# Packed attention steps, and four changed borders, in a hybrid encoder step on one core

## The chip, the cores and the metric

The program runs on one core of one Trainium2 chip. The metric is device time in microseconds (us) for one execution of the whole program. One execution was profiled; the others were only timed.

## The reference

One layer of a streaming encoder for 1024 prompt frames and 8 x 16 sample frames (T = 1152 columns) of width 1024, in f32. What matters here:

```
z = rmsnorm(x, g_mix) @ w_in            # cq, ckv, kpe, rq, rk, rv, rg, sq, sk, sv
o_mla = softmax(q k^T * scale, chunk-causal) @ v          # 8 heads, 96 wide
o_ret = retention(rq, rk, rv); ret_y = head_norm(o_ret) * silu(rg)
# stick-breaking, 4 heads of 64:
z_ = q k^T / 8;  before = k_pos < q_pos
log_keep = where(before, log_sigmoid(-z_), 0)
a = where(before, exp(log_sigmoid(z_) + reverse_exclusive_cumsum(log_keep)), 0);  o_sb = a @ v
x = x + concat(o_mla, ret_y, o_sb) @ w_out
x = x + memory_attend(rmsnorm(x), 256 memory tokens, 4 heads of 128)
x = x + conv_ffn(rmsnorm(x));  y = rmsnorm(x)
```

The sample frames have caches of 512 past frames (MLA latents, stick-breaking keys and values) and their own memory keys and values.

## The kernel before

Everything lies features by frames in on-chip memory: 8 or 18 blocks of 128 features, each over 1152 frames. A product with weights is made as three fp32r products (high part with high part, high with low, low with high), in chunks of 384 frames (`CH`, `NCH` = 3); a projection of one block is 3 chunks of 24 products. Each engine has its own list of instructions, in an order written out by hand; semaphores join the lists. Weights stream in 512 KB slots through two buffers: SyncE (SP) loads, GpSimd (POOL) splits into high and low parts (L749, L752), TensorE (PE) multiplies (L1751 in `split_products`, L1829 in `first_projection`), VectorE (DVE) evacuates.

**Input projection.** 18 blocks in the order `IN_ORDER`; block n goes to banks 3(n mod 2) + c. `z_chunk` (L1263, L1268) evacuates. The last four blocks hold the stick-breaking queries and values of one head each. After the last block, `stick_breaking_tokens` (L1960) transposes the values by tiles into banks 4 to 7.

**Prompt attention.** `STEPS` lists steps for two heads at a time: 2 x 8 stick-breaking steps `("sb", pair, tile)`, then four MLA passes of 8 steps `("mla", pass, tile)`, with four sample steps `("sbs", ...)` set between MLA steps by `SB_S_AFTER`. Step j handles the 128 queries of tile j against the 128(j + 1) keys up to it, so that its width grows from 128 to 1024 columns. S[0] and S[1] (two PSUM banks each, banks 0 to 3) hold the scores of the first and the second head; banks 4 and 5 take the transposes, bank 6 the output, bank 7 the projections. In iteration t:

- TensorE: scores (L1976 sb, L1979 mla, L1992 and L1995 sample) and the transposes of step t - 1 (L2009), first head, then second head; then a projection chunk for a later pass (L2049, L2052, L2056, L2061, `project_chunk`); the values of step t - 2 (L2031, sample L2026); further chunks. `STEP_CHUNKS` says which chunks stand in which iteration: eleven for each pass, made during the pass before, and those of pass 0 during stick-breaking. The chunks share bank 7, so each waits until the one before is evacuated.
- VectorE: for sb a mask on the last 128 columns (L1430), then, when ScalarE has written the sigmoids, a reversed running product (scan, L1456) and a product (L1459); for mla a memset of the hidden corner (L1445), the row maximum (L1447), a reciprocal and a scaling (L1466, L1468); copies of transposes (L1477), query chunks (L1490).
- ScalarE: two sigmoids (L931, L932; sample L940, L941) or the exponential (L949), copies of the transposes (L959), outputs into `mixed` (L967, L973, L977), other chunks (L1001, L1002, L1006).

`kbuf` (the 1 - sigmoid part) is single for each head, `prob` double. In iteration 2 (`KPE_STEP`) the rotary key is turned (L1421, ScalarE L913, L1424). SP loads the mask `hide`, then `rope_pe` and `w_pass` after the last input block, stores sk and sv, loads the sample caches (L658, L659; each waits until the values of the sample step before are done), and later the MLA latents.

**Sample MLA.** Eight steps, one for each sequence (L2095, L2096, L2104, L2113; VectorE L1537 to L1547, ScalarE L1044 to L1059), then the head products L2119 and a copy into `mixed` (L1063).

**Output projection.** ScalarE rounds the eight blocks of `mixed` (L1072), VectorE makes the remainders (L1552), and `first_projection` (L1829) takes them block by block as they come.

**Memory attention.** Twelve steps (`N_MEM`): eight prompt tiles with four heads (scores L2152, values L2174), four pairs of sample sequences (scores L2160, values L2182: 16 products of 16 columns), transposes L2194. VectorE: maximum L1592, remainder of the output L1598, copy L1606, reciprocal and scaling L1609, L1612. ScalarE: exponentials L1101, copies L1111, rounding L1135, sample queries L1126 into `qm_pair`, which VectorE clears once (L1586) before the loop. `memory_output(m, c)` makes block m, chunk c of the projection behind it from 12 products; two chunks stand in iteration N_MEM - 1, and 22 after the loop.

```python
            pe.wait_ge(g_evac, G_MO)
            pe.wait_ge(qm_zero, 1)
            for n in range(N_MEM + 2):
```

## Time and profile before

| | |
|---|---|
| runs, us | 1861.46, 1866.43, 1856.43 (median 1861.46) |
| profiled execution: its own time | 1855.89 us |
| its span | 1854.1 us, mean granted TensorE clock 0.976 |
| TensorE busy | 1779.7 us (96%), 10471 products |
| VectorE, ScalarE, GpSimd busy | 1084.6 (58%), 552.7 (30%), 490.6 us (26%) |
| chain that ended last | TensorE 87%, VectorE 8%, ScalarE 3%, issue 2% |
| input projection ends | 325.6 us |
| first output product | 720.5 us |
| memory attention begins | 877.4 us |
| last memory output product | 1007.9 us |

A group in the profile is a line, an engine, an operation and its tiles, with count, busy time, the mean of one and the idle time before it. The chain of waits is followed back from the last instruction. Products overlap, so that a busy TensorE is not one at its peak. An f32 product counts as two records, an fp32r product or a transpose as one.

### The profile page before, as it was taken

How to read it: one execution, taken by the hardware profiler on the slowest of the kernel's cores; microseconds unless marked ns; L12 is line 12 of the kernel's file. 1: busy time of each engine (PE TensorE's matmuls, PEld its weight loads, DVE VectorE, ACT ScalarE, POOL GpSimd, SP SyncE). 2: the span in 40 equal slices, each digit the busy share in tenths (PEclk: the TensorE clock that was granted, in tenths of full speed). 3: DMA queues.
4: the chain of work that ended last, by engine and by line, in shares of the span. 5: the costliest groups of instructions: out<-in, count | busy, mean ns of one | idle time of the engine just before them, and what ended most of it. 6: DMA issues, size and time to landing. Idle time of an engine off the chain costs nothing.

```text
span 1854.1 us, 26688 instructions
## 1 busy us (share of the span) xinstructions
PE 1779.7 (96%) x10471; PEld 1615.7 (87%) x10471; DVE 1084.6 (58%) x1519; ACT 552.7 (30%) x1037; POOL 490.6 (26%) x219
## 2 busy tenths in 40 slices
PE   7999999898998998999999999999999999999997
PEld 7998899455655757998899999999999999999987
DVE  7754365677445665443627766656555565565577
ACT  7211110566554644110513312121121121211234
POOL 2851121000000011433003433333333333233331
PEclk9999899899999999999989999999999999999999
DMA  5330110501111311331421111111111111111112
GB/s 212 92 109 12 60 41 17 159 10 48 58 46 46 119 47 41 133 123 38 190 110 46 35 46 45 45 34 45 45 35 44 45 45 34 45 45 34 46 44 102
DMA packets 34974, 119.29 MB, mean 64 GB/s; under 512 B 4944, under 2 KB 7984, under 8 KB 32464
## 3 DMA queue, kind: packets, MB, share of 16 engines
q1 hardware_dynamic: 32592, 108.76, 17.9%
q10 hardware_dynamic: 2304, 9.44, 1.5%
q8 instruction: 56, 0.92, 0.2%
q14 instruction: 22, 0.18, 0.0%
HBM read 100.73 MB, written 15.17 MB: 63 GB/s over the span
## 4 chain that ended last, share of the span: by engine, by line
PE 87%; DVE 8%; ACT 3%; issue 2%; DMA 0%; ACTq 0%; DVEq 0%; SPq 0%
PE scores L1751 33%; PE bank L1751 31%; PE scores L1979 3%; PE scores L1829 2%; PE bank L2009 2%; DVE kbuf L1456 2%; PE bank L2031 2%; PE bank L2049 2%; PE bank L2182 1%; PE bank L2026 1%; DVE prob L1459 1%; PE scores L1773 1%; PE scores L2160 1%; PE bank L1760 1%; PE scores L1992 1%
## 5 line engine op out<-in xcount | busy, mean ns | idle before, releaser
L749 POOL TENSOR_TENSOR w_hi<-w_raw,zero 128x1024 fp32r<-128x1024 f32 x96 | 186.9, 1947 | 1292.9 <-PE bank L1751 570.2
L1751 PE MATMUL scores<-act_hi,w_hi 128*128 128x384 f32 x976 | 330.5, 339 | 0.0
L1751 PE MATMUL scores<-act_lo,w_hi 128*128 128x384 f32 x976 | 328.7, 337 | 0.0
L1751 PE MATMUL scores<-act_hi,w_lo 128*128 128x384 f32 x976 | 328.7, 337 | 0.0
L752 POOL TENSOR_TENSOR w_lo<-w_raw,w_hi 128x1024 fp32r<-128x1024 f32 x96 | 250.1, 2606 | 7.6
L1751 PEld LDWEIGHTS scores<-act_hi,w_hi 128*128 128x128 f32 x976 | 184.2, 189 | 0.6 <-issue 0.2
L1751 PEld LDWEIGHTS scores<-act_lo,w_hi 128*128 128x128 f32 x976 | 184.2, 189 | 0.3 <-issue 0.2
L1751 PEld LDWEIGHTS scores<-act_hi,w_lo 128*128 128x128 f32 x976 | 184.1, 189 | 0.0
L1679 DVE TENSOR_TENSOR x<-bank,x 128x384 f32<-128x384 f32 x216 | 120.4, 558 | 103.6 <-PE bank L1751 103.6
L1751 PE MATMUL bank<-act_hi,w_hi 128*128 128x384 f32 x512 | 172.2, 336 | 0.0
L1751 PE MATMUL bank<-act_hi,w_lo 128*128 128x384 f32 x512 | 172.0, 336 | 0.0
L1751 PE MATMUL bank<-act_lo,w_hi 128*128 128x384 f32 x512 | 172.0, 336 | 0.0
L1653 DVE SCALAR_TENSOR_TENSOR conv<-ext,consts,conv 128x1168 f32<-128x1168 f32 x44 | 117.5, 2671 | 79.4 <-ACT conv L1152 79.4
L1751 PE MATMUL bank<-s_hi,w_hi 128*128 128x384 f32 (+2 forms) x454 | 153.0, 337 | 0.0
L1751 PE MATMUL bank<-s_lo,w_hi 128*128 128x384 f32 (+2 forms) x454 | 152.7, 336 | 0.0
L1751 PE MATMUL bank<-s_hi,w_lo 128*128 128x384 f32 (+2 forms) x454 | 152.6, 336 | 0.0
L1163 ACT ACTIVATE s_hi<-conv 128x1024 fp32r<-128x1024 f32 x20 | 21.2, 1061 | 344.1 <-DVE conv L1662 344.1
L2009 PEld LDWEIGHTS bank<-ident,prob 128*128 128x128 f32 x452 | 54.4, 147 | 51.8 <-DVE prob L1459 23.0
L1751 PEld LDWEIGHTS bank<-act_hi,w_hi 128*128 128x128 f32 x512 | 96.3, 188 | 0.2
L1751 PEld LDWEIGHTS bank<-act_lo,w_hi 128*128 128x128 f32 x512 | 96.3, 188 | 0.0
L1751 PEld LDWEIGHTS bank<-act_hi,w_lo 128*128 128x128 f32 x512 | 96.3, 188 | 0.0
L2009 PE MATMUL bank<-ident,prob 128*128 128x128 f32 x452 | 73.3, 291 | 15.6 <-DVE prob L1459 11.2
(341 smaller groups left out, 3377.7 us busy)
## 6 DMA issues: line engine op xcount, KB each, us to landing
w_raw<-wstream SPq DMA_DIRECT2D x108, 512.0 KB, 3.5
x_blk<-xT ACTq DMA_DIRECT2D x8, 576.0 KB, 4.6
x_mid<-x_blk ACTq DMA_DIRECT2D x8, 576.0 KB, 3.1
x<-x_mid SPq DMA_DIRECT2D x4, 1152.0 KB, 6.5
z<-cache_k SPq DMA_DIRECT2D x4, 1024.0 KB, 5.2
z<-cache_v SPq DMA_DIRECT2D x4, 1024.0 KB, 7.2
mk_c<-mk_c SPq DMA_DIRECT2D x4, 1024.0 KB, 11.5
mv_c<-mv_c SPq DMA_DIRECT2D x4, 1024.0 KB, 13.5
```

Source lines behind the costliest of these rows:

```text
L749: pool.tensor_tensor(w_hi[:, k], w_raw[:, k], zero[:].unsqueeze(2).to_broadcast([P, KB, P]), ALU.add).then_inc(w_rounded, 1)
L752: pool.tensor_tensor(w_lo[:, k], w_raw[:, k], w_hi[:, k].bitcast(F32), ALU.subtract).then_inc(w_split, 1)
L1163: act.activation(dst[:, 0:TP], conv[:, 0, 0:TP], ACT.Copy)
L1456: own_v(dve.tensor_tensor_scan(keep[:, ::-1], keep[:, ::-1], ones[:, 0:1].to_broadcast([P, width]), 1.0, ALU.mult, ALU.mult))
L1653: own_v(dve.scalar_tensor_tensor(c, ext[:, ab, 1:EXT - 1], conv_tap(m + NFF * ab, 1), c, ALU.mult, ALU.add))
L1679: dve.tensor_tensor(x[:, m, frames(c)], bank[6 + q % 2][:, 0:CH], x[:, m, frames(c)], ALU.add).then_inc(d_evac, 1)
L1751: mm = pe.matmul(out, w[:, k, at + kb], x(kb), start=first and kb == 0 and n == 0, stop=last and kb == n_kb - 1 and n == 2)
L1829: mm = pe.matmul(bank[c][:, 0:CH], w[:, 0, kb], x[:, kb, frames(c)], start=kb == 0 and n == 0, stop=kb == KB - 1 and n == 2)
L1979: mm = pe.matmul(S[hh][:, at:end], q_pass[i % 2][:, hh, tile(j)], k_pass[i % 2][:, hh, at:end], start=True, stop=True)
L2009: mm = pe.transpose(bank[4 + g % 2][:, tile(b)], prob[:, t % 2, hh, tile(4 * k + b)], ident[:])
L2031: mm = pe.matmul(bank[6][64 * hh:64 * hh + 64, 0:P], v, probT[:, t % 2, hh, tile(b)], start=b == 0, stop=b == j)
L2049: mm = pe.matmul(bank[7][:, 0:CH], w_pass[:, s, (2 * hh + kb) * P:(2 * hh + kb + 1) * P], z[:, Z_CQ + kb, frames(k)], start=kb == 0, stop= ...
```

## The change

Five things. (1) An attention step takes one or two tiles, up to 8 blocks of 128 keys: `PACKS` is (7), (6, 0), (5, 1), (4, 2), (3). A pair or a pass has 5 steps instead of 8. The tiles of a step lie side by side in S, and row maximum, exponential, scan, product and scaling are issued for each tile by itself; transposes, their copies, the mask and the memset for the step. The chunks and the sample steps are set anew, a chunk can also stand between the heads. (2) The first stick-breaking step is tile 3 of pair 0; its scores stand between chunks 0 and 1 of input block 16, whose banks become 6, 7 and 1. Its sigmoids lie in `kbuf0` and `prob0`, and `hide` is loaded ahead of the last input weights, into the place of `bd`. (3) Blocks 6 and 7 of `mixed` are rounded during the sample MLA, and the output projection starts with them. (4) The clearing of `qm_pair` moves into iteration 2 of the memory loop. (5) The value products of the four sample pairs are issued between the products of four chunks of the memory output, (0, 1), (1, 0), (0, 0), (1, 1).

```diff
-    return (0, 1, 4)[c] if n in RET_BLOCKS else 3 * (n % 2) + c
+    return (0, 1, 4)[c] if n in RET_BLOCKS else (6, 7, 1)[c] if n == NZ - 2 else 3 * (n % 2) + c
...
+MIX_ORDER = (6, 7, 0, 1, 2, 3, 4, 5)
+MIX_AFTER = {4: 6, 6: 7}
+MO_CHUNKS = [(0, 1), (1, 0), (0, 0), (1, 1)]
+MO_CHUNKS += [(m, c) for m in range(KB) for c in range(NCH) if (m, c) not in MO_CHUNKS]
...
-SB_S_AFTER = {(0, 4): 0, (1, 1): 1, (1, 6): 2, (2, 3): 3}
-STEPS = [("sb", p, j) for p in range(2) for j in range(NTILE)]
+PACKS = ((7,), (6, 0), (5, 1), (4, 2), (3,))
+SB_S_AFTER = {(0, 2): 0, (1, 0): 1, (1, 3): 2, (2, 1): 3}
+STEPS = [("sb", p, tiles) for p in range(2) for tiles in (PACKS[4:] + PACKS[:4] if p == 0 else PACKS)]
...
 for _n in range(NCK):
-    STEP_CHUNKS[3 + _n].append((0, _n))
+    STEP_CHUNKS[2 + _n // 2][_n % 2 + 1].append((0, _n))
     for _i in range(1, NP):
-        STEP_CHUNKS[FIRST[_i - 1] + min(7, (_n + 1) * 2 // 3)].append((_i, _n))
+        _steps = [_t for _t in range(FIRST[_i - 1], END[_i - 1]) if STEPS[_t][0] == "mla"]
+        STEP_CHUNKS[_steps[(_n + 1) // 3]][(_n + 1) % 3].append((_i, _n))
...
+        hide = Region(at_bd, 512)("hide", [P, P])
+        kbuf0 = Region(at_pair[0] + 17408, 4096)("kbuf0", [P, 2, 512])
+        prob0 = Region(at_pair[1] + 4608, 4096)("prob0", [P, 2, 512])
...
+                if slot == W_OUT - 1:
+                    sp.wait_ge(sum_used, Q_HEAD + 6)
+                    sp.dma_start(hide[:], io["before"][:, 1]).then_inc(hide_in, 16)
                 sp.wait_ge(w_split, slot - 1)
                 load_weights(slot)
...
             sp.wait_ge(w_used, W_OUT)
-            sp.dma_start(hide[:], io["before"][:, 1]).then_inc(hide_in, 16)
...
 # ScalarE
+            act.wait_ge(ret_done, 2)
+            for hh in range(2):
+                sb_sigmoids(0, hh)
+            act.wait_ge(w_used, W_OUT)
+            act.wait_ge(lora_normed, 3)
+            act.wait_ge(g_evac, NZ * NCH)
+            sb_sigmoids(1, 0)
+            stick_breaking_values(0)
+            stick_breaking_values(2)
+            copy_groups(0, 0)
+            stick_breaking_values(4)
+            sb_sigmoids(1, 1)
+            copy_groups(0, 1)
...
+                for n, (_, at, w) in enumerate(spans(t)):
+                    last = act.activation(prob[:, t % 2, hh, at:at + w], S[hh][:, at:at + w], ACT.Exp,
+                                          bias=neg_max[:, k + n:k + n + 1], accum_out=row_sum[:, k + n:k + n + 1])
...
+                    if b in MIX_AFTER:
+                        act.wait_ge(stored_skv, 128)
+                        round_mixed(MIX_AFTER[b])
...
-            for kb in range(KB):
-                act.activation(mix_hi[:, kb], mixed[:, kb], ACT.Copy).then_inc(mix_rounded, 1)
+            for kb in MIX_ORDER[2:]:
+                round_mixed(kb)
...
 # VectorE
+            dve.wait_ge(hide_in, 16)
+            z_chunk(NZ - 2, 0)
+            mask(0, 0)
+            mask(0, 1)
+            z_chunk(NZ - 2, 1)
+            finish(0, 0)
+            z_chunk(NZ - 2, 2)
+            finish(0, 1)
+            z_evacuate(NZ - 1)
+            for t in range(1, N_STEPS + 2):
...
                 if heads:
                     mask(t, 0)
+                if t == 1:
+                    stick_breaking_values(1)
+                    stick_breaking_values(3)
                 if copied:
                     copy_groups(t - 1, 0)
                 if heads == 2:
                     mask(t, 1)
+                for chunk in STEP_CHUNKS[t][0]:
+                    evacuate_chunk(*chunk)
                 if heads:
                     finish(t, 0)
                 if copied == 2:
                     copy_groups(t - 1, 1)
-                for chunk in STEP_CHUNKS[t][:1]:
+                for chunk in STEP_CHUNKS[t][1]:
                     evacuate_chunk(*chunk)
                 if heads == 2:
                     finish(t, 1)
...
+                if n == DB - 1:
+                    split_mixed(0)
+            for i in range(1, KB):
+                split_mixed(i)
...
-            for k in range(2):
-                dve.wait_ge(xb_out[k], 16 * KB // 2)
-            dve.memset(qm_pair[:], 0.0).then_inc(qm_zero, 1)
             for n in range(N_MEM + 3):
...
+                if n == 2:
+                    for k in range(2):
+                        dve.wait_ge(xb_out[k], 16 * KB // 2)
+                    dve.memset(qm_pair[:], 0.0).then_inc(qm_zero, 1)
                 if n < N_MEM:
                     dve.wait_ge(m_exp, n + 1)
...
 # TensorE
+            input_chunk(NZ - 2, 0)
+            pe.wait_ge(g_evac, NCH * (NZ - 2))
+            for hh in range(2):
+                scores(0, hh)
+            input_chunk(NZ - 2, 1)
+            input_chunk(NZ - 2, 2)
+            input_block(NZ - 1)
+            pe.wait_ge(g_evac, NCH * (NZ - 1))
+            scores(1, 0)
+            pe.wait_ge(g_evac, NCH * NZ)
+            for g in range(4):
+                value_tokens(g)
+            scores(1, 1)
+            pe.wait_ge(sv_copied["act"], 2)
+            value_tokens(4)
+            pe.wait_ge(sv_copied["dve"], 1)
+            for hh in range(2):
+                transposes(0, hh)
...
+            for t in range(2, N_STEPS + 2):
                 for hh in range(2):
                     if t < N_STEPS and hh < n_heads(t):
                         sample_scores(t) if STEPS[t][0] == "sbs" else scores(t, hh)
                     if 1 <= t <= N_STEPS and hh < n_heads(t - 1):
                         transposes(t - 1, hh)
-                for chunk in STEP_CHUNKS[t][:1]:
-                    project_chunk(*chunk)
+                    for chunk in STEP_CHUNKS[t][hh]:
+                        project_chunk(*chunk)
                 if t >= 2:
                     values(t - 2)
...
-            first_projection(W_OUT, G_OUT - 2 * NCH, mix_split, 0, mix_hi, mix_lo)
+            first_projection(W_OUT, G_OUT - 2 * NCH, mix_split, 0, mix_hi, mix_lo, MIX_ORDER)
...
+            def sample_values(c, i):
+                if i < 5:
+                    sample_value(c, 2 * i)
+                    sample_value(c, 2 * i + 1)
+                else:
+                    sample_value(c, i + 5)
...
-            pe.wait_ge(qm_zero, 1)
...
+                        memory_output(*MO_CHUNKS[c - NTILE], lambda i: sample_values(c, i))
...
-                if n == N_MEM - 1:
-                    memory_output(0, 0)
-                    memory_output(0, 1)
-            for n in range(2, KB * NCH):
-                memory_output(n // NCH, n % NCH)
+            for m, c in MO_CHUNKS[DB // 2:]:
+                memory_output(m, c)
```

`spans(t)` gives for each tile of a step its number, its first column in S and its width; `between` is called behind each of the first eleven of a chunk's twelve products. `sample_value(c, i)` issues product i of the sixteen.

## Rows read from the trace of the kernel before

**Rows 1.** Windows: stretch, length, busy us (x) of PE, PEld, DVE, ACT, POOL, PEclk, DMA, GB/s

```profile
325.60:385.20 59.60, 49.32 (x238) 26.79 (x238) 44.52 (x60) 34.13 (x71) 0.00 (x0) 0.84 0.44 124
...
385.20:443.50 58.30, 52.61 (x333) 33.13 (x333) 40.60 (x59) 39.89 (x91) 0.00 (x0) 0.90 0.13 46
...
443.50:636.60 193.10, 179.80 (x1177) 120.56 (x1177) 101.81 (x249) 104.32 (x246) 0.00 (x0) 0.97 0.15 51
...
636.60:675.90 39.30, 36.75 (x296) 24.83 (x294) 28.52 (x64) 22.05 (x55) 8.96 (x4) 1.00 0.35 121
...
926.90:1007.90 81.00, 79.83 (x456) 78.04 (x455) 39.67 (x53) 19.72 (x27) 13.89 (x6) 0.89 0.23 83
```

**Rows 2.** Chain of waits in stick-breaking: start us, us, what

```profile
366.79 0.22 DVE scores L1430
...
368.79 2.04 DVE kbuf L1456
...
385.21 1.97 PE bank L2009 x8
...
437.62 1.97 PE bank L2009 x8
```

**Rows 3.** Chain of waits in the memory attention and its output

```profile
875.50 1.78 DVE qm_pair L1586
...
926.97 3.46 PE scores L2160 x16
...
935.25 5.70 PE scores L2160 x16
...
940.96 3.48 PE bank L2182 x32
...
944.70 4.17 PE scores L1751 x24
...
953.04 6.72 PE bank L2182 x32
...
960.50 5.81 PE scores L1751 x24
```

**Rows 4.** Groups by form, 325.6 to 720.5 us: VectorE and ScalarE in stick-breaking

```profile
L1456 DVE TENSOR_TENSOR_SCAN kbuf<-kbuf,ones 128x1024 f32<-128x1024 f32 x4 | 9.1, 2286 | 3.6 <-ACT prob L932 3.6
...
L1430 DVE TENSOR_TENSOR scores<-scores,hide 128x128 f32<-128x128 f32 x32 | 8.9, 295 | 10.1 <-PE scores L1976 10.0
...
L1459 DVE TENSOR_TENSOR prob<-prob,kbuf 128x1023 f32<-128x1023 f32 x4 | 4.9, 1224 | 0.1
...
L932 ACT ACTIVATE prob<-scores 128x1024 f32<-128x1024 f32 x4 | 4.2, 1045 | 0.0
```

**Rows 5.** Chain of waits in the MLA passes, TensorE

```profile
492.64 1.73 PE scores L1979 x4
...
499.79 1.29 PE bank L2049 x4
...
507.23 1.71 PE scores L1992 x4
...
509.38 1.34 PE scores L1992 x3
...
529.44 4.41 PE bank L2026 x40
...
627.06 0.77 PE bank L2009 x7
...
637.93 1.90 PE bank L2031 x32
```

**Rows 6.** DMA issues, 488 to 500 us: KB each, us to landing

```profile
z<-cache_v SPq DMA_DIRECT2D x1, 1024.0 KB, 7.2
```

**Rows 7.** Chain of waits at the output projection

```profile
715.12 1.12 PE bank L2119 x16
...
720.51 14.61 PE scores L1829 x72
```

More of the change, by code:

```diff
@@ L1520, in _ @@
                     finish(t, 1)
-                for chunk in STEP_CHUNKS[t][1:]:
+                for chunk in STEP_CHUNKS[t][2]:
                     evacuate_chunk(*chunk)
@@ L1746, in _, with split_products @@
         def _(pe):
-            def split_products(out, k, at, n_kb, hi, lo, first=True, last=True, weights=(w_hi, w_lo)):
+            def split_products(out, k, at, n_kb, hi, lo, first=True, last=True, weights=(w_hi, w_lo), between=None):
                 for kb in range(n_kb):
```

264 lines of the change are left out of this document (141 added, 123 removed).

## The prediction

> **What bounds the kernel now.** I read the windows by stage first, then the chain of waits in order of time, then the groups by form for the price of one instruction, and last the DMA issues. In the windows the reader is to see that TensorE is busy nearly everywhere, so a gain has to come from one of three places: TensorE idle, TensorE running at its lower level, or TensorE busy with work that could lie under something else. Outside the stretch from 325.6 to 1007.9 us the change touches nothing.
>
> The stretch splits in four. (a) Stick-breaking, 325.6 to 443.5 us: TensorE is idle for 10.3 us and then 5.7 us, and its mean granted clock is 0.84 and 0.90 [rows 1]. The chain there runs through VectorE: mask, then two sigmoids on ScalarE, then scan and product [rows 2]. (b) The MLA passes with four sample steps between them, 443.5 to 675.9: 232.4 us, 216.6 of them busy, clock 0.97 and 1.00. (c) The seam between the sample MLA and the output projection, around 715 to 735. (d) The memory attention and its output projection, to 1007.9: TensorE counts as busy for 79.8 of the last 81.0 us, but at a mean clock of 0.89 [rows 1]; the sample scores of a step take 3.46 us in one place and 5.70 in the next, and one group of value products 3.48 and then 6.72 [rows 3]. So in (d) it is the clock and the short products that cost.
>
> **Stick-breaking, packed.** A pair of heads goes through 36 blocks of 128 keys for each head either way. Before, these are 8 steps; after, 5 (8, 8, 8, 8 and 4 blocks). Columns, scans, products and score matmuls stay the same in number. One full width costs VectorE 2.286 (scan) + 1.224 (product) us and ScalarE 1.045 us for each of two sigmoids [rows 4]. For a pair: 36 blocks are 4.5 full widths, times two heads, times 3.51, is 31.6 us; the extra instructions of narrow tiles (about 0.3 us for each tile and head beyond 4.5, an estimate from the 0.295 us of a 128-column operation [rows 4]) bring 33.8. Each step also has an opening that VectorE cannot fill: mask 0.3, hand-over 0.1, the first head's two sigmoids; the row pair 366.79 to 368.79 shows 2.0 us at 896 columns [rows 2]. Eight openings are 8 x 0.4 + 2 x (4.5 x 1.045 + 3.5 x 0.17) = 13.8 us, five are 2.0 + 9.6 = 11.6. So the sum is 47.6 before, 45.4 after. But the second pair took 385.21 to 437.62, 52.4 us [rows 2]: 4.8 us more than the sum, the latency of its narrow first steps behind the widest step of the pair before. Steps of even width should lose most of that: 6 us gained in the second pair, from the first scan on.
>
> The first pair: its 512-column step moves between chunks of block 16. What moves: on TensorE two heads of scores, 2 x 0.87 = 1.7 us, which now lengthen the input projection; on VectorE two masks, two scans and products (2 x 1.9 us), among evacuations of 1.1 us every 4.2 us, so hidden; on ScalarE four sigmoids and the table load, where it was waiting anyway. On SP the mask's load is moved ahead of the last weight load: 64 KB, hidden because that load is waiting for its split anyway; if it were not, TensorE would wait for the last weights by the load's few us at most. What is left behind the projection is the last evacuation (1.1 us), the 1024-column step's scores and the value transposes, then a rotary key of 4 us on VectorE as before. I work the first pair out as 45.4 - 5.5 (the moved step) + 3.5 (start) + 4 (rotary) + 6 x 0.55 (query evacuations) + 1.7 = 52.4 against 59.6 now: 7 us. The chunks of pair 0 now start one step earlier and wait for the stores of sk and sv; I put that at 0 to 3 us. A second charge: TensorE at half speed just after the border, which now meets a full step instead of narrow ones; 0 to 5 us. Stage (a): 6 + 7 - 2 = **11 us**, bounds 0 and 16.
>
> **The MLA passes, packed.** TensorE's own work in a full step is scores 2 x 1.73, sixteen transposes at 0.11 and values 1.90 = 7.1 us; a pass is 4 x 7.1 + 3.6 = 32.0 [rows 5]. A query chunk is 1.29; the five others of a pair 0.86 or less by their columns; eleven make 11.8, for three pairs 35.4. A sample step is 1.71 + 1.34 + 5 x 0.11 + 4.41 = 8.0, four are 32 [rows 5]. Sum 4 x 32.0 + 35.4 + 32 = 195 us against 232.4 measured: 37 us are latency and clock. Narrow steps (2 to 6 blocks) have too little TensorE work to cover mask, exponential and scaling of the same step; a packed step has 7.1 us of it. What stays: with three chunks in a step, the second waits for VectorE to evacuate the first behind the second head's mask, about 1.2 us, twice a pass, 7 us in all; the last pass without chunks is near VectorE's own 6.5 to 7.5 us a step, 3 us; sample steps with their two table loads of 1.28 us, 1 to 2 us each instead of about 5; clock and hand-overs 4 to 6. That leaves about 216: **16 us**, bounds 4 (only the sample steps gain) and 28.
> What is late next: the cache of a sample step is loaded after the values of the one before, and lands 7.2 us after its issue [rows 6]. Now only one step lies between the two, 8.8 to 10 us of TensorE's work by the prices above. It fits by 1 to 2 us; if it does not, up to 3 us for each of three loads.
>
> **The seam before the output projection.** Now the products start at 720.51, after the head products of 715.12 (1.12 us), the copy, and the first rounding and its remainder [rows 7]. After, two of eight blocks are ready and TensorE can start at 716.3. Two blocks last 2 x 1.56 = 3.1 us (12.5 us for eight at full clock); the third is ready at 720.4 as the first is now; six more last 9.4, so the end is 729.9 instead of 720.51 + 14.61 = 735.12: **5 us**, bounds 3 and 6. The two roundings move into the sample MLA on ScalarE (1.15 us each), which has over 2 us free in a step of 4.6; the remainder (1.37) behind VectorE's last scaling may delay a copy, 0 to 0.5 us.
>
> **Memory attention.** The memset of 1.78 us that TensorE waits for [rows 3] goes; it comes back in VectorE's queue in the third step, where VectorE and ScalarE set the pace. I charge it in full there; left is that TensorE starts without the stop: **1 us**, 0 to 3. Then the sample values: 16 products of 16 columns cost 3.48 us at full clock, 0.109 for each of 32 weight loads, and 12 products of 384 columns 2.08 (24 in 4.17) [rows 3]. Interleaved, a weight load can lie under each long product: 11 x 0.109 = 1.2 us a group, 4.8 for four. The low clock now costs (5.70 - 3.46) + (6.72 - 3.48) + (5.81 - 4.17) = 7.1 us [rows 3]. With long products in between, I expect some two thirds of that back: **10 us** together, bounds 0 (loads do not overlap between short and long, clock as before) and 13. Two chunks already filled this place, so only two are new there. Weights: the first block is split before the loop begins; VectorE's sums keep their order, with the counts moved.
>
> Sum: 11 + 16 + 5 + 1 + 10 = **43 us**. The profiled execution took 1855.9 us for a span of 1854.1; it is at the lower end of the runs (median 1861.5), so 1813 by its own time, and about 1817 to 1818 beside the median. A change within 0.5%, 9 us, would not be told from none.
>
> **A rule against it.** The same transposes cost 0.11 us each (seven in 0.77) and, behind the widest stick-breaking step, 0.25 (eight in 1.97) [rows 2, 5]: they run at either level of the clock, 1.2 or 2.4 GHz, and the lower one came where TensorE had waited for VectorE's scan. The Trainium skill (TensorE: Matmul & The Clock Gate, Part 4: PE-mode transpose) says that transposes do not count as TensorE activity and that the full clock does not engage for them. The trace disagrees as to the full clock; whether they count, no row here shows. By that rule the packed stick-breaking steps, with their transposes in long runs between waits, would invite the lower level, which leads to the slower rival below.
>
> **The rivals.**
> 1. *Forecast*, 1807 to 1828, chance 0.50.
> 2. *The latency stays*: packed steps only join waits, because masks, chunk evacuations and table loads stand in the same order on VectorE and ScalarE, and the memory loop keeps its low clock. Stage (a) 6, (b) 7, seam 4, memory 5: 22 us, about 1840. For it: VectorE is in the chain of the wide steps too [rows 2]. Chance 0.25.
> 3. *More*: every cover holds, 14 + 25 + 6 + 14 = 59 us, 1802. Against it: the waits between chunks. Chance 0.12.
> 4. *The gain goes*: the caches land late (9 us), the stores hold the first chunks (3), nothing in memory: about 1856. Chance 0.06.
> 5. *Slower: TensorE's clock falls in the packed stick-breaking steps.* At 1.2 GHz a full step needs 2 x 7.1 + 2 us of chunks = 16.3 against VectorE's 11.2: +5 us in each of eight steps, 41 us; with the four full steps of the last pass (14.2 against 7.6) 26 more. Net 43 - 67: 24 us slower, 1885. It decides once the mean clock in such a step is under (7.1 + 1.2)/11.2 = 0.74. Against it: 0.84 and 0.90 now, and packed steps give TensorE more work between waits. Chance 0.07.
> That the change does nothing can be excluded: the steps, and the order of products, are written out.
>
> **How the numbers follow.** The likeliest case gives 1817. Low 1797 takes in the third case; high 1846 takes in the second; outside are the last two and the edges. Faster by over 0.5%: 0.50 + 0.25 + 0.12, less a little at the edge, 0.86; within, 0.07; slower 0.07.
>
> **What would show it.** Stick-breaking from the end of the input projection to the last scan should be about 99 us instead of 112, with a step of 1024 columns every 10 to 11.5 us and the mean clock not under 0.84. The MLA stage should be 216 us or less, with TensorE idle under 8 us. The first output product should start within 0.2 us of the head products' end, with one wait of about 1 us before the third block. The interleaved groups should take about 4.4 us each and no stretch among them show a clock near 0.5. I am wrong if a sample score waits for the cache's DMA, if a packed step has TensorE at the lower level and VectorE idle, or if a group of short and long products takes 5.5 us or more.

## The result, and the profile after

The changed kernel takes 1840.9 us (median; 1836.8 to 1844.3) against 1863.7 for the kernel before in the same runs: ratio 0.9893, 95% interval 0.9867 to 0.992. By the ratio that is some 20 us faster: inside the range, but less than half of the 43 that the sum gave. The profiled execution took 1842.4 us for a span of 1840.6; the kernel before had a span of 1854.1. These 13.5 us are made up so: the stretch of the change gained 21.1; the input projection was already 3.3 us behind where the change first touches it; and what follows the memory output, where nothing was changed, took 4.3 more, at a lower mean clock (0.94 over the last 150 us against 0.98).

The windows by stage of the changed kernel (columns as in [rows 1]):

```profile
330.16:425.59 95.43, 84.64 (x536) 54.84 (x535) 74.00 (x89) 61.82 (x108) 0.00 (x0) 0.95 0.32 93
425.59:661.17 235.58, 216.64 (x1502) 149.70 (x1502) 134.50 (x277) 121.23 (x290) 8.80 (x4) 0.99 0.19 67
...
700.40:715.34 14.94, 14.04 (x89) 13.55 (x90) 9.27 (x9) 7.04 (x7) 0.00 (x0) 1.00 0.25 80
...
854.79:907.36 52.57, 46.72 (x291) 41.96 (x292) 33.54 (x45) 27.39 (x116) 4.24 (x2) 0.94 0.42 171
907.36:990.13 82.77, 81.67 (x456) 79.79 (x455) 36.44 (x52) 19.66 (x27) 16.42 (x6) 0.88 0.23 81
```

The first line answers to the first two of [rows 1]: the clock is 0.95 instead of 0.84 and 0.90. The second answers to the next two: 235.6 us for passes and sample steps against 232.4, TensorE idle for 18.9 us against 15.8. (These windows begin with the first scores of the passes, which now start 1.0 us before the last stick-breaking product ends and started 5.9 after it before. So the table below counts the passes from that product.) The last one answers to the last: 82.8 us against 81.0, at 0.88 against 0.89. Set against the terms, each as lengths of the stage:

| term | forecast gain, us | measured, us |
|---|---|---|
| stick-breaking, to its last product | 11 | 112.0 to 96.4, less 1.3 that the projection grew: 14.3 |
| passes, from that product | 16 | 238.3 to 234.6: 3.7 |
| seam, from the head products to the end of the first output block | 5 | 20.0 to 14.9: 5.1 |
| memset | 1 | 2.2 gained before the loop, 2.4 lost in it: -0.2 |
| interleaving and its clock | 10 | -1.9 |

The stick-breaking product and scan are VectorE's (L1534 and L1529 here); "to" and "from" it mean its end. Three stretches of the chain of waits in the passes show what the second term met (start us, us, what):

```profile
438.66 1.74 PE scores L2081 x6
...
440.48 0.17 DVE scores L1516
...
440.72 0.97 issue
441.69 0.28 DVE neg_max L1519
441.97 0.47 DVE q_pass L1568
...
442.49 0.59 PE bank L2152
...
498.17 0.60 PE bank L2111 x4
...
499.40 0.82 ACT L991
...
500.70 0.70 ACT prob L991
501.40 0.60 ACT prob L992
...
502.03 1.50 DVE prob L1529
...
503.55 0.83 DVE prob L1534
...
504.43 0.93 PE bank L2111 x5
...
640.94 1.14 issue
642.08 2.50 DVE prob L1545
644.57 0.60 DVE probT L1555
...
645.28 3.82 DVE prob L1545 x2
...
649.14 0.68 PE bank L2111 x4
```

First, TensorE waits 2.08 us (440.40 to 442.49) for VectorE to evacuate a query chunk behind mask and maximum; this is in the chain six times. In four of the six, transposes run under 0.87 us of it, and 1.2 us are idle; in the other two TensorE is idle for 2.1. That is 9.2 us in all. Second, a sample step: 5.66 us from 498.77 to 504.43 for table load, two sigmoids, scan and product. Third, the end of the last pass: 9.93 us from 639.23 on. There GpSimd is at work, in the timeline of its engine (start us, us, what):

```profile
641.88 2.47 POOL L812 TENSOR_TENSOR w_lo<-w_raw,w_hi 128x1024 fp32r<-128x1024 f32 x1
644.32 2.01 POOL L809 TENSOR_TENSOR w_hi<-w_raw,zero 128x1024 fp32r<-128x1024 f32 x1
646.40 2.47 POOL L812 TENSOR_TENSOR w_lo<-w_raw,w_hi 128x1024 fp32r<-128x1024 f32 x1
```

And the groups by form give the price of the same scaling, up to 636 us and after (busy us, mean ns):

```profile
L1545 DVE TENSOR_SCALAR prob<-prob,row_sum 128x384 f32<-128x384 f32 x6 | 2.5, 415 | 0.0
...
L1545 DVE TENSOR_SCALAR prob<-prob,row_sum 128x384 f32<-128x384 f32 x2 | 5.0, 2492 | 0.0
```

A scaling of 384 columns that costs 415 ns takes 2492. The one at 642.08 ends at 644.57, just after GpSimd's operation of 641.88 has ended at 644.35. In the memory attention, two lines of the chain and the group after them:

```profile
871.63 1.76 DVE qm_pair L1705
...
907.36 3.46 PE scores L2296 x16
910.99 0.35 PE bank L2268 x4
911.34 0.27 PE scores L1849
...
916.21 0.27 PE scores L1849
916.70 3.46 PE scores L2296 x16
```

The memset is back in the chain, in the third iteration, for 1.76 us. The woven group of 16 short and 12 long products lasts from 910.82 to 916.48, 5.66 us at full clock. Apart they are 3.48 + 2.08 = 5.56 by [rows 3]; 4.4 was forecast.

### The profile page after: what moved, and what is told of

The parts are those of the page before. It is cut to its first block, busy times and chain, and to the rows that moved or that the text cites. A ratio compares the mean times of both kernels' runs of the same rounds, so it can differ in the third digit from the quotient of the medians.

```text
span 1840.6 us, 26432 instructions
## 1 busy us (share of the span) xinstructions
PE 1771.5 (96%) x10471; PEld 1621.2 (88%) x10471; DVE 1079.3 (59%) x1459; ACT 538.9 (29%) x977; POOL 493.7 (27%) x219
## 4 chain that ended last, share of the span: by engine, by line
PE 89%; DVE 6%; ACT 2%; issue 2%; DMA 0%; ACTq 0%; DVEq 0%; SPq 0%
PE scores L1849 33%; PE bank L1849 32%; PE scores L2081 3%; PE bank L2111 2%; PE bank L2134 2%; PE scores L1929 2%; PE bank L2152 2%; PE scores L2078 1%; DVE kbuf L1529 1%; PE bank L2128 1%; PE scores L1873 1%; PE bank L1860 1%; PE scores L2296 1%; PE scores L2094 1%; PE bank L2268 1%
## 5 line engine op out<-in xcount | busy, mean ns | idle before, releaser
L1849 PE MATMUL scores<-act_hi,w_hi 128*128 128x384 f32 x960 | 325.2, 339 | 0.0
L1849 PE MATMUL scores<-act_lo,w_hi 128*128 128x384 f32 x960 | 323.5, 337 | 0.0
L1849 PE MATMUL scores<-act_hi,w_lo 128*128 128x384 f32 x960 | 323.4, 337 | 0.0
L1849 PE MATMUL bank<-act_hi,w_hi 128*128 128x384 f32 x528 | 177.7, 337 | 0.0
L1849 PE MATMUL bank<-act_hi,w_lo 128*128 128x384 f32 x528 | 177.4, 336 | 0.0
L1849 PE MATMUL bank<-act_lo,w_hi 128*128 128x384 f32 x528 | 177.4, 336 | 0.0
L1751 DVE SCALAR_TENSOR_TENSOR conv<-ext,consts,conv 128x1168 f32<-128x1168 f32 x44 | 117.5, 2671 | 79.4 <-ACT conv L1227 79.4
L1753 DVE SCALAR_TENSOR_TENSOR conv<-ext,consts,conv 128x1168 f32<-128x1168 f32 x44 | 84.3, 1916 | 5.7 <-DVE conv L1751 3.0
L1849 PEld LDWEIGHTS bank<-s_hi,w_hi 128*128 128x128 f32 x454 | 85.4, 188 | 0.4
```

The source lines that it names most:

```text
L1751: own_v(dve.scalar_tensor_tensor(c, ext[:, ab, 1:EXT - 1], conv_tap(m + NFF * ab, 1), c, ALU.mult, ALU.add))
L1753: dve.scalar_tensor_tensor(c, ext[:, ab, 2:EXT], conv_tap(m + NFF * ab, 2), c, ALU.mult, ALU.add).then_inc(conv_done, 1)
L1849: mm = pe.matmul(out, w[:, k, at + kb], x(kb), start=first and kb == 0 and n == 0, stop=last and kb == n_kb - 1 and n == 2)
```

## The experiments

All but the last three change the changed kernel in one respect. The stages are taken from one profile of each, by the same starts each time: the passes from the last stick-breaking product (VectorE's) to the last value product of the passes, the memory part from the first sample value to the last product of the projection behind the memory output. The kernel before has 238.7 and 89.8. Where the text gives gains in us for a whole kernel "by the ratios", it is the difference of two ratios times the 1859 us of the kernel before in those runs.

| kernel | ratio to before, 95% | passes, us | memory part, us |
|---|---|---|---|
| changed | 0.9893 (0.9867 to 0.992) | 234.4 | 91.5 |
| e7, passes single | 0.9915 (0.9896 to 0.9934) | 234.7 | 91.4 |
| e8, stick-breaking single | 0.996 (0.9946 to 0.9974) | 232.7 | 91.4 |
| e9, roundings late | 0.9925 (0.9896 to 0.9954) | 233.9 | 96.3 |
| e4, split late | 0.9856 (0.9825 to 0.9887) | 228.1 | 96.0 |
| e5, chunk slots | 0.9839 (0.9796 to 0.9883) | 227.8 | 96.0 |
| e6, sample places | 0.9852 (0.9814 to 0.9889) | 229.8 | 96.3 |
| e3, memset early | 0.9869 (0.9831 to 0.9906) | 235.5 | 96.0 |
| e1, values alone | 0.9858 (0.9837 to 0.9878) | 234.3 | 87.8 |
| e2, blocks | 0.9896 (0.9877 to 0.9915) | 232.2 | 86.5 |
| b1, all, values alone | 0.9774 (0.9747 to 0.9801) | 217.5 | 89.5 |
| b2, all, blocks | 0.9782 (0.9758 to 0.9806) | 217.7 | 91.3 |
| e10, b1's memory part and split, passes single | 0.9849 (0.9817 to 0.9882) | 233.3 | 89.8 |

**Passes in single tiles.**

```diff
-SB_S_AFTER = {(0, 2): 0, (1, 0): 1, (1, 3): 2, (2, 1): 3}
+SB_S_AFTER = {(0, 4): 0, (1, 1): 1, (1, 6): 2, (2, 3): 3}
...
-    for _k, _tiles in enumerate(PACKS):
+    for _k, _tiles in enumerate((_j,) for _j in range(NTILE)):
...
-        STEP_CHUNKS[_steps[(_n + 1) // 3]][(_n + 1) % 3].append((_i, _n))
+        _slots = STEP_CHUNKS[FIRST[_i - 1] + min(7, (_n + 1) * 2 // 3)]
+        _slots[2 if _slots[1] else 1].append((_i, _n))
```

> The changed kernel with the MLA passes back in single tiles (8 steps a pass), their chunks and the sample steps where they stood before; stick-breaking stays packed. Measured is the stretch from the last stick-breaking product to the end of the last pass's values (238.3 us in the kernel before, 234.6 in the changed one). Theory A (the packed steps save hardly anything, since TensorE's own work of some 195 us now lies wholly on the chain and about 40 us of waits remain, while before some 30 us of that work lay under the waits): the stretch becomes 235 to 240 us, the kernel 0 to 5 us slower than the changed one, so 1841 to 1846. Theory B (the forecast: packing is worth 16 us there, and something else in the changed kernel, such as the steps' new place behind stick-breaking, took it away again): the stretch grows by 10 us or more, the kernel to about 1851 to 1857.

The stretch is 234.7 us in single tiles and 234.4 packed, and the ratios differ by 0.0022, 4 us, with intervals that overlap. As the change places its chunks and sample steps, packing is worth between nothing and 4 us: theory A.

**Stick-breaking in single tiles.**

```diff
-STEPS = [("sb", p, tiles) for p in range(2) for tiles in (PACKS[4:] + PACKS[:4] if p == 0 else PACKS)]
+STEPS = [("sb", p, (j,)) for p in range(2) for j in ((3, 7, 0, 1, 2, 4, 5, 6) if p == 0 else range(NTILE))]
...
-    STEP_CHUNKS[2 + _n // 2][_n % 2 + 1].append((0, _n))
+    STEP_CHUNKS[3 + _n][1].append((0, _n))
```

> The changed kernel with stick-breaking back in single tiles (8 steps a pair; the 512-column step still first and still between the last two blocks of the input projection, the 1024-column one behind it, then 128, 256, ... in order); the MLA passes stay packed. Measured is the time from the end of the input projection to the last stick-breaking product: 112.0 us in the kernel before, 96.4 in the changed one. Theory A (the forecast's working: the packing gives 6 us in the second pair and, with the moved step worth most of the first pair's 7, another 1 to 4 in the first): 103 to 107 us here, the kernel 7 to 10 us slower than the changed one. Theory B (the moved step alone did it, the packed steps only join waits): 96 to 99 us, 0 to 3 slower. Theory C (packing did nearly all): 108 to 112, 12 to 16 slower.

From the projection's end to the end of the last product it is 109.2 us (329.5 to 438.7), and the kernel is 12.5 us slower than the changed one (0.0067 of 1859). That is theory C, not the forecast's A: of the 15.6 us that the change gained here, packing gives 12.8 and the moved step the rest. The windows of the two, changed kernel and then this one:

```profile
332.00:426.00 94.00, 83.21 (x532) 54.46 (x532) 73.26 (x88) 62.18 (x110) 0.00 (x0) 0.95 0.32 93
```

```profile
331.40:437.40 106.00, 92.09 (x526) 55.33 (x526) 75.85 (x99) 67.70 (x151) 0.00 (x0) 0.90 0.30 92
```

VectorE's own work is 2.6 us less when packed; the other 9.4 us are its idle time, 30.1 against 20.7. TensorE's mean clock is lower as well in single tiles, 0.90 against 0.95. How much of the idle time goes back to that, and how much to the latency of narrow steps, isn't separated here.

**Roundings of two blocks late.**

```diff
-MIX_AFTER = {4: 6, 6: 7}
+MIX_AFTER = {}
...
-            for kb in MIX_ORDER[2:]:
+            for kb in MIX_ORDER:
...
-                if n == DB - 1:
-                    split_mixed(0)
-
-            for i in range(1, KB):
+
+            for i in range(KB):
                 split_mixed(i)
```

> The changed kernel with the early rounding of two blocks undone: blocks 6 and 7 are rounded and split behind the head products with the rest, in the same order of products. The seam from the end of the sample MLA's head products to the end of the first output block's products was 20.0 us before and 14.9 after. Theory A (the forecast: those two blocks give TensorE 3.1 us to work on while the third is made ready, and the start is 1.2 us of rounding and 1.4 of remainder earlier): 19 to 20.5 us again, the kernel 4 to 6 us slower than the changed one. Theory B (the gain came from elsewhere, such as the clock): 15 to 17 us, within 2.

From the head products' start to the start of the last product of the first block it is 20.2 us (699.84 to 720.0) instead of 14.6, and the kernel is 6 us slower: theory A. The order alone is worth nothing; the two early blocks are worth the forecast's 5 us.

Part of these 5 us is the clock. The 72 products of the first block take 15.15 us here and 14.61 in the kernel before, and at full clock 12.5. The window of the kernel before:

```profile
720.51:735.12 14.61, 14.61 (x73) 14.61 (x74) 9.67 (x9) 5.85 (x6) 0.00 (x0) 0.86 0.07 27
```

In both kernels the lower level came while TensorE stood idle, for 4.3 us, before the first product; in the changed kernel, where it starts at once, the window shows 1.00. So some 3 us of the 5.1 are the wait, and 2.1 (14.61 - 12.5) the clock.

**GpSimd's split late.**

```diff
             sp.wait_ge(q_evac, evacuated(NP - 1, NCK - 1, "dve"))
+            sp.wait_ge(p_ready, N_ITEMS)
```

> The changed kernel with one wait added on SP's queue: the weights of the output projection are loaded only once VectorE has scaled the last pass, so GpSimd splits them beside the sample MLA and not beside the last packed steps. In the changed kernel's chain VectorE's two scalings of the last full step take 3.67 and 3.81 us while GpSimd splits, and TensorE waits 9.93 us for them and runs at the lower level afterwards. Theory A (GpSimd slows VectorE): the scalings take under 1.2 us, the wait at the end of the last pass is 3 to 5 us, and the kernel is 6 to 9 us faster than the changed one, so about 1833, provided the weights are still in time for the output projection. Theory B (the wait is the last pass's own latency, since no chunks fill it): the scalings stay over 3 us or the wait stays over 8, and the total within 2 us. Theory C (the weights come too late): the first output products start 2 us or more later after the head products.

6.3 us off the passes, and 6.9 off the kernel by the ratios: theory A. Of the 9.93 us at the end of the last pass no wait over 1 us is left, where theory A had left 3 to 5. In its groups by form from 628 us on the scaling has its price again:

```profile
L1546 DVE TENSOR_SCALAR prob<-prob,row_sum 128x512 f32<-128x512 f32 x2 | 1.0, 487 | 0.1
L1546 DVE TENSOR_SCALAR prob<-prob,row_sum 128x384 f32<-128x384 f32 x2 | 0.8, 414 | 0.0
```

The output projection starts no later behind the last value product (41.1 us both times).

**Chunk slots.**

```diff
-        STEP_CHUNKS[_steps[(_n + 1) // 3]][(_n + 1) % 3].append((_i, _n))
+        _at = ((0, 1), (0, 2), (1, 1), (1, 2), (2, 1), (2, 2), (3, 0), (3, 1), (3, 2), (4, 0), (4, 1))[_n]
+        STEP_CHUNKS[_steps[_at[0]]][_at[1]].append((_i, _n))
```

> The changed kernel with the chunks of a pass in other slots: no packed step has a chunk between its two heads' scores and transposes and another right behind in the place where the second has to wait for VectorE to evacuate the first. In the changed kernel this wait of 2.08 us is in the chain six times, 0.87 of it being transposes that have to run anyway: 1.2 us net, 7 in all. Theory A (the wait is taken out): six waits fewer in the chain, the stretch of the passes 5 to 7 us shorter, the total too. Theory B (the latency moves: the mask and the exponential of the second head end the next wait instead, or the last chunk's evacuation delays the next pass's first scores): the stretch within 2 us of the changed kernel's 234.6.

6.6 us off the passes: theory A. None of the six waits of 2.08 us is left. In two of the passes a wait of 3.68 us stands where two of them were (4.18 in a third), as at 438.89 in its chain:

```profile
438.97 0.18 DVE scores L1517
...
439.17 1.29 DVE neg_max L1520 x2
...
441.45 0.60 DVE probT L1556
442.05 0.48 DVE q_pass L1569
...
442.57 1.56 PE bank L2153 x4
```

The chain alone would not show a gain, as the longer waits are as long in sum. But TensorE works under them; under the one shown run eight transposes, a chunk and 16 value products, and 0.5 us is idle. In all, TensorE's idle time in the stretch is 12.6 us (227.8 less 215.2 busy), against 18.6 (234.4 less 215.8).

**Places of the sample steps.**

```diff
-SB_S_AFTER = {(0, 2): 0, (1, 0): 1, (1, 3): 2, (2, 1): 3}
+SB_S_AFTER = {(0, 1): 0, (1, 1): 1, (2, 0): 2, (2, 3): 3}
```

> The changed kernel with the four stick-breaking sample steps further from each other and from the pass borders: behind the second, second, first and fourth steps of the passes rather than the third, first, fourth and second. What is measured is whether the caches' loads or the neighbours' width set the wait at these steps. In the changed kernel they cost 1 to 2 us of TensorE idle each net of its own work. Theory A (place matters: behind full steps only): 2 to 5 us faster. Theory B (two table loads and a 640-column scan make the wait wherever the step stands): within 2 us.

4.6 us off the passes, at the upper end of theory A. Two steps still show the full wait of 5.67 us (555.88 and 602.54), the other two now none over 1.5.

**Memset in the first iteration.**

```diff
-                if n == 2:
+                if n == 0:
```

> The changed kernel with VectorE's zeroing of the query pairs in the first iteration of the memory loop, where VectorE waits for the exponentials anyway, rather than in the third. In the changed kernel the chain runs through this operation for 1.76 us in the third iteration. Theory A (it stands in VectorE's queue where VectorE sets the pace): the operation is out of the chain and the stretch from the loop's first scores to the last prompt values 1.5 to 2 us shorter (51.5 in the changed kernel, 49.6 to 51.5 in others of its kind, by the clock). Theory B (VectorE had time): the same stretch, another operation in the chain in its place.

Theory A: the operation is out of the chain, and the stretch from first scores to last prompt values is 48.2 us, against 51.5 in the changed kernel and 49.1 before. Kernels that leave the memset in the third iteration have 49.6 to 51.5, by the clock, so less than the whole 3.3 us is its own. The total can't show it: its four runs scatter over 18 us (1825.7 to 1844.0).

**Sample values by themselves.**

```diff
-MO_CHUNKS = [(0, 1), (1, 0), (0, 0), (1, 1)]
+MO_CHUNKS = []
...
-                        memory_output(*MO_CHUNKS[c - NTILE], lambda i: sample_values(c, i))
+                        for i in range(11):
+                            sample_values(c, i)
...
+                if n == N_MEM - 1:
+                    memory_output(0, 0)
+                    memory_output(0, 1)
...
-            for m, c in MO_CHUNKS[DB // 2:]:
+            for m, c in MO_CHUNKS[2:]:
```

> The changed kernel with the last of its parts undone: the sample values of the memory attention run by themselves again, the chunks of the memory output in plain order, two of them in the last iteration as before. Measured is the stretch of the four groups, 80.9 us before, 82.8 after, and the clock in it, 0.89 before. Theory A (the interleaving saves nothing: what the weight load of a short product gains under a long one, the long one's own load loses, and the lower clock only shifts): the stretch is 80 to 82 us, the kernel 1 to 3 us faster than the changed one. Theory B (the forecast: interleaving saves 4.8 us of loads and some clock, hidden by a loss elsewhere in the stretch): the stretch is 85 us or more, the kernel 3 us or more slower.

3.7 us off the memory part, and the kernel 6.5 us faster than the changed one by the ratios: theory A, and beyond its 1 to 3. In the profiles, 2.8 us more lie in the input projection and 3.0 behind the memory part, where the two kernels are alike, so the edit is shown for the 3.7 only.

**Values and chunk as blocks.**

```diff
-                        memory_output(*MO_CHUNKS[c - NTILE], lambda i: sample_values(c, i))
+                        for i in range(11):
+                            sample_values(c, i)
+                        memory_output(*MO_CHUNKS[c - NTILE])
```

> The changed kernel with the same order of chunks and of sample values, but each set of 16 short products ahead of its chunk of 12 long ones, as two blocks, rather than woven together. At full clock the two together are 3.48 + 2.08 = 5.56 us by the rows of the kernel before; woven they took 5.66. Theory A (no load is hidden on balance): 5.5 to 5.7 us for the two at full clock, and the stretch of four groups within 1 us of the changed kernel's 82.8, the total within 1 us. Theory B (weaving does save loads, 0.109 us for each of 11): 6.7 us for the two at full clock or 4 to 5 us more for the stretch. Theory C (short products in one run draw the lower clock, which the weaving prevents): the clock of the stretch falls below the changed kernel's 0.86, and the stretch grows by 2 us or more with the pair still at 5.56 where the clock is full.

Its chain, one group at full clock:

```profile
907.24 3.48 PE bank L2268 x32
910.72 2.19 PE scores L1849 x12
```

5.67 us in blocks, 5.66 woven: on loads, weaving saves nothing. The memory part is 5 us shorter than woven in the profile, so none of the three theories has it whole: A is right on the loads and wrong on the stretch, and C has the clock the wrong way round. The total doesn't bear the 5 us out: the six runs go from 1830.9, the profiled one, to 1841.9, and the ratio is that of the changed kernel.

Over all profiles: the eight kernels with woven groups have a memory part of 91.4 to 96.3 us, the six without (the kernel before among them) 86.5 to 91.3. The longest stretch at the lower level of the clock, 0.50, in the changed kernel, in e4, in e1 and in e2 (windows):

```profile
929.50:950.00 20.50, 19.84 (x77) 19.02 (x77) 1.77 (x5) 0.72 (x3) 0.00 (x0) 0.50 0.15 47
```

```profile
914.20:944.90 30.70, 29.60 (x117) 28.34 (x116) 2.76 (x9) 1.17 (x5) 0.00 (x0) 0.50 0.21 80
```

```profile
926.60:940.30 13.70, 12.53 (x51) 12.20 (x50) 2.36 (x6) 1.19 (x4) 0.00 (x0) 0.50 0.37 134
```

```profile
925.60:932.40 6.80, 6.37 (x24) 5.90 (x24) 0.49 (x2) 0.45 (x2) 0.00 (x0) 0.50 0.00 0
```

TensorE is busy nearly throughout the memory part, so each microsecond at the lower level costs half of one. With that half taken off, nothing is left of the differences (us):

| kernel | memory part | longest at 0.50 | all at 0.50 | part less half of that |
|---|---|---|---|---|
| changed (woven) | 91.4 | 20.5 | 20.5 | 81.2 |
| e4 (woven) | 96.0 | 30.7 | 30.7 | 80.7 |
| before | 89.8 | 10.2 | 17.1 | 81.3 |
| e1, values alone | 87.8 | 13.7 | 13.7 | 81.0 |
| e2, blocks | 86.5 | 6.8 | 10.2 | 81.4 |
| b2, all, blocks | 91.3 | 6.8 | 20.5 | 81.0 |

All 14 profiles have 80.6 to 81.4 us in the last column. So the order of short and long products costs or saves nothing by itself that these 0.8 us would show; what differs is the time at the lower level, 20.5 to 30.7 us in the eight woven kernels and 10.2 to 20.5 in the six others. e2 and b2 have the same order and differ by 10 us of it, so one profile of a kernel doesn't settle its share.

**All together.** The edits of e3, e4, e5 and e6, with those of e1 (b1) or of e2 (b2):

> The changed kernel with five of its choices altered at once: the interleaving undone, the memset in the memory loop's first iteration, GpSimd's split of the output projection's first weights behind the last scaling, the chunks in their new slots, the stick-breaking sample steps at their new places. Alone, the split, the slots and the places took 6.3, 6.6 and 4.6 us off the stretch of the passes (234.4 us from the last stick-breaking product to the last value product), and the undone interleaving took 3.6 us off the end of the memory attention. If they add up, the stretch is 217 us, which is what the forecast gave the packed passes (216 or less from the first scores), the memory part is 5 us shorter, and the kernel 20 us faster than the changed one: 1820 (ratio to the kernel before 0.979). If they overlap (the same wait taken out twice, the next one behind it): 226 to 229 us for the stretch and 1829.

> The same kernel as the one before, but with sample values and chunk as two blocks in each of the four groups, rather than all sample values by themselves and two chunks in the last iteration. Theory A (what matters is TensorE's clock in the stretch, and the less of the 16-column products stand close together the better): 0 to 5 us faster than the other. Theory B (the shorter the short products' stretch in all, the less time at the lower level): 2 to 6 us slower than the other, as the two stood to each other on the changed kernel (1838 against 1833).

They add up: the passes take 217.5 and 217.7 us (234.4 less 6.3, 6.6 and 4.6 is 216.9), and the medians are 1818.0 and 1818.5 us beside 1859.3 for the kernel before, 22 us faster than the changed kernel for b1. Between the two there is no difference that the runs can tell. One cost came back in b1: from the last value product to the first output product 46.1 us instead of 41.1. The split now meets the first scaling of the sample MLA, as chain and GpSimd's timeline show:

```profile
649.63 2.39 DVE prob L1648
...
649.32 2.34 POOL L814 TENSOR_TENSOR w_lo<-w_raw,w_hi 128x1024 fp32r<-128x1024 f32 x1
```

That scaling is 0.56 elsewhere in this chain. In b2 the same scaling takes 2.37 us, but the stretch only 43.0: its clock is 1.00 there, and b1's 0.93 (0.69 from 650 to 661 us). So the meeting costs 1.8 us, and 3 of b1's 5 go with the lower level.

**Single passes beside the best.** The edits of e1, e3 and e4 with the passes in single tiles, chunks and sample steps where the kernel before had them:

> The first of the two combined kernels (values by themselves, memset early, GpSimd's split late) with the MLA passes in single tiles again, their chunks and sample steps where the kernel before had them; stick-breaking stays packed. In the changed kernel the packing of the passes was worth nothing (234.4 us packed, 234.7 single). Theory A (packing pays once its own slots are set right, so that a packed step's 7 us of TensorE work covers one latency instead of two): the stretch is 228 to 230 us here against 217.5 packed, the kernel 10 to 12 us slower than that one, about 1829. Theory B (the slots and places, not the packing, made the gain, and the split's delay helps single tiles as much or more): the stretch is 217 to 224, the kernel within 6 us of that one.

233.3 us against 217.5 packed, and 14 us slower by the ratios (0.0075 of 1859): theory A, with more than it expected, since the late split took only 1.4 us off single tiles. The windows of the passes in b1 and then in e10:

```profile
425.90:643.40 217.50, 211.18 (x1500) 146.83 (x1498) 128.59 (x276) 120.19 (x288) 0.33 (x1) 1.00 0.19 67
```

```profile
426.00:659.30 233.30, 218.95 (x1500) 147.97 (x1498) 131.36 (x324) 129.99 (x312) 0.00 (x0) 0.98 0.18 63
```

Of the 15.8 us, 8.0 are idle time of TensorE (14.4 against 6.3), and 7.8 a longer busy time for the same 1500 products, at 0.98 of the clock instead of 1.00. The comparison isn't one of packing alone. Each side has its own chunk slots and sample places, and only the packed side had its places improved by a trial: in e10's chain all four sample steps show a wait of 5.7 to 6.1 us, 23.4 in all, in b1's two of 5.67, 11.3 in all. Single tiles with the sample steps behind their widest tiles weren't tried. What is shown is that packing together with its slots and places is worth 16 us against the kernel before's arrangement, and that without them it is worth 0 to 4.

## Why the prediction was wrong

The second rival, "the latency stays", gave the total (1840), but not its parts: it has 6, 7, 4 and 5 us for stick-breaking, passes, seam and memory, and measured were 14.3, 3.7, 5.1 and -2.1. That the totals agree is chance. Against the forecast's 43, the passes lack 12 us and the interleaving 12, and stick-breaking gave 3 more.

**Stick-breaking** held: the first pair took 49.5 us (330.16 to 379.7; forecast 52.4), the second 46.9 (forecast 52.4 - 6), and to the last product it was 96.4 for "about 99". The share of the parts was off: packing gave 12.8 us (e8), where the working has 2.2 from the sum and 4.8 from latency for one pair. The slower rival, with a clock under 0.74, is refuted by 0.95.

**The passes are the step that failed**, in its list of "what stays". The list gave 21 us over the 195 of TensorE's own work; measured were 40.6 (235.6 - 195). The 195 itself was low. A sample step's scores are priced 1.71 + 1.34, but the chain of the kernel before goes from 507.23 to 511.15, 3.92 us: the products with the sample's own columns are left out, 0.9 us a step, 3.5 in all. And [rows 1] has TensorE busy for 216.6 of the 232.4 us, so that only 15.8 were idle, where the working calls 37 us "latency and clock". The forecast's 216 for the stage is within 2 us of what b1 reaches, and its 16 for packing is the 15.8 between e10 and b1; but b1 has three edits more that the forecast didn't foresee, so the agreement is in part luck. Three entries of the list were wrong or incomplete:
- *The last pass, "3 us"*: it cost 9.93 us and a run of values at the lower clock (3.61 us for 32 products at 651.70, 1.90 elsewhere), because GpSimd splits the first output weights over VectorE's scalings. The forecast had no entry for it, though the kernel before shows the same in its groups by form: 2016 ns for 768 columns, between 686 for 896 and 554 for 640. Taken out: 6.3 us.
- *The sample steps, "1 to 2 us each"*: 16.7 us of chain in all, 5.66 at two of them. Their places alone are worth 4.6 us (e6); where a wait is left, its pieces are table load, two sigmoids, scan and product. The caches, which the forecast feared, were in time: no sample score waits for their DMA.
- *The waits between chunks, "1.2 us, twice a pass, 7 in all"*: right in place and number; they cost 9.2 us of idle time, and e5 won 6.6. But they belonged to the slots, not to packing.

Beside this, the waits in the kernel before had been doing work: TensorE's pieces in the chain were 174.6 us before, 193.6 after. Some 20 us of its work lay beside other engines' pieces and came into the chain as the waits went. TensorE's busy time shows nothing of it: 216.6 before, 216.6 after, by [rows 1] and the windows above. The Trainium skill (Perfetto Trace Analysis, Identifying the Most-Contended Engine) calls matmul busy time no good measure of how close a kernel is to the roofline, as pipelined instructions look smaller in the trace. The trace agrees that it is no good measure; but here the records look larger: a product of 384 columns is recorded with 336 ns, while one starts every 173.

**The seam** held: start of the products at once, the third block ready at 705.7, 5.1 us (e9: 5.6). The working sets 12.5 us for eight blocks at full clock against a measured 14.61, so 2.1 of its 5 us were a gain of clock that it didn't name; the clock did come back.

**The memset** was charged in full, and was: 2.2 us gained before the loop, 2.4 lost in it. What the forecast missed is the free place two iterations earlier (e3).

**The interleaving** failed too, on "a weight load can lie under each long product: 1.2 us a group". The records' starts show a gain on one side and a loss on the other. A short product behind a long one costs 0.13 us instead of 0.22, two of them 0.35 instead of 0.44; but a long product behind a short one costs 0.27 instead of 0.173. A likely reading is that the long product's own load, which had lain under the long product before it, is now bare beside the short one. The group of 5.66 us has one long product at 0.17 and eleven at 0.27, 3.1 us for 2.08, and short ones for 2.5 us that took 3.48: 1.06 lost, 0.95 gained. The 5.67 in blocks says the same. "Some two thirds of the low clock back" had no row behind it, and the clock went the other way: 20.5 us at the lower level in the memory part instead of 17.1, and up to 30.7 in other woven kernels. The prediction's own test, a group of 5.5 us or more, told it.

Open: why the lower level lasts longer in the woven kernels. Open too is the clock behind the memory part, which makes up to 4.3 us between profiles of kernels that are alike there. That b1 would gain another 2 to 5 us with a split that meets no scaling at all wasn't tried.

## What to carry to other kernels

In this kernel, packing narrow MLA steps paid only with the small work re-placed around it: list each wait that the new order makes, with its place in the queue, before counting the gain. Look in the trace for one operation of unusual length (by form, not by mean), and ask who ran beside it. To hide a weight load, count the loads that lose their cover too.

## What was unexpected of the hardware

VectorE's scaling doesn't slow down beside GpSimd's split; it stands until the split's instruction ends. At 384 columns it takes 415 ns alone and 2492 beside the split, and it ended 0.22 us after GpSimd's instruction, both times; at 640 columns (b1 and b2) it was 0.35 us, at 768 (the kernel before, twice) 0.41. The Trainium skill (SBUF — State Buffer, Who interferes with whom) has that rule: the two engines share a pair of ports, and a tensor_scalar that runs in a two-port mode and a GpSimd operation exclude each other for the whole instruction. The traces agree, in the changed kernel, in b1 and b2, and with 2016 ns for 768 columns in the kernel before; e4 shows it gone with the overlap.

And TensorE ran through 20.5 us at 0.50 of the clock in the changed kernel, and through 30.7 in e4, while its records show it busy for 19.84 and 29.60 of them, and its weight loads for 19.02 and 28.34. In the changed kernel's stretch these are short and long products in turn, but for two transposes. A busy TensorE in the records was no protection from the lower level.
